# Wide expert rounds in blocks of 512, 1024, 1024 and 1024 inner columns, with extra and light tokens multiplied together

## What is computed

```python
def moe_swiglu(h, w_router, b_router, w1, w3, w2):
    logits = (h @ w_router) + b_router
    top_val, top_idx = lax.top_k(logits, TOP_K)          # TOP_K = 2
    top_w = softmax(top_val)
    gate = einsum('blk,blke->ble', top_w, one_hot(top_idx, N_EXPERTS))
    out = 0
    for e in range(N_EXPERTS):                            # 8
        out += gate[..., e:e + 1] * ((silu(h @ w1[e]) * (h @ w3[e])) @ w2[e])
    return out
```

## Time and profile before

| what | value |
|---|---|
| runs, median (3 runs) | 2324.79 us (2324.08 to 2325.15) |
| profiled execution, span from first to last instruction | 2321.8 us |
| profiled execution, time of its own | not given apart from the span; the median lies 3.0 us above the span |
| TensorE busy | 2176.6 us (94%) |
| TensorE weight loads | 1533.7 us (66%) |
| VectorE, ScalarE busy | 1193.5 us (51%), 788.2 us (34%) |
| DMA, mean rate | 278 GB/s |
| mean granted TensorE clock | 0.984 |
| loads of expert weights | 336 of 1024 KB, median 13.6 us from issue to landing |

### The profile page before, as it was taken

How to read it: one execution, slowest core, us unless ns; L and a number is a source line. 1 busy time by engine, 2 the same in 40 slices (tenths; PEclk the granted TensorE clock), 3 DMA queues, 4 the chain that set the end, 5 groups by cost and what they waited for, 6 DMA issues and landing times.

```text
span 2321.8 us, 40892 instructions
## 1 busy us (share of the span) xinstructions
PE 2176.6 (94%) x17031; PEld 1533.7 (66%) x17031; DVE 1193.5 (51%) x1899; ACT 788.2 (34%) x1195; POOL 223.8 (10%) x257
## 2 busy tenths in 40 slices
PE   7998999999988899999998999999999999889998
PEld 2974679976422233237776776687769987546997
DVE  3727847646501001015545464485557668984663
ACT  2511744433000000014344443344545542104552
POOL 1006310001000000000000000000000054660000
PEclk9998999999899999999999999999999999999999
DMA  9529387767999999999999999974667556505552
GB/s 344 171 90 290 86 294 247 281 210 289 388 415 407 414 403 409 414 404 355 394 394 363 346 394 392 378 229 147 221 215 253 182 192 226 236 10 183 191 190 73
DMA packets 254874, 645.38 MB, mean 278 GB/s; under 512 B 12831, under 2 KB 103136, under 8 KB 234600
## 3 DMA queue, kind: packets, MB, share of 16 engines
q1 hardware_dynamic: 248508, 629.93, 74.0%
q0 software_dynamic: 5904, 12.36, 2.1%
q10 hardware_dynamic: 284, 0.54, 0.1%
HBM read 641.72 MB, written 1.05 MB: 277 GB/s over the span
## 4 chain that ended last, share of the span: by engine, by line
PE 68%; DMA 19%; DVE 8%; issue 3%; ACT 1%; POOL 0%; SPq 0%; DVEq 0%; ACTq 0%; POOLq 0%
DMA ring<-in_moe_w 17%; PE bank L2003 6%; PE bank L2004 6%; PE bank L2005 6%; PE bank L2013 5%; PE bank L2015 5%; PE bank L2014 5%; PE bank L1039 3%; PE bank L887 3%; PE bank L1040 2%; PE bank L1041 2%; PE bank L1971 2%; PE bank L1949 2%; DVE arena L1761 2%; PE bank L933 2%
## 5 line engine op out<-in xcount | busy, mean ns | idle before, releaser
L1479 DVE TENSOR_TENSOR w_low<-ring,w_high 128x1024 fp32r<-128x1024 f32 x168 | 198.8, 1221 | 192.5 <-ACT w_high L1205 192.4
L3071 DVE TENSOR_TENSOR ring_low<-ring,up_high 128x1024 fp32r<-128x1024 f32 x186 | 224.7, 1265 | 115.9 <-ACT up_high L2628 115.6
L1205 ACT ACTIVATE w_high<-ring 128x1024 fp32r<-128x1024 f32 x168 | 170.0, 1054 | 246.7 <-DMA ring<-in_moe_w 216.6
L2628 ACT ACTIVATE up_high<-ring 128x1024 fp32r<-128x1024 f32 x186 | 182.6, 1046 | 85.1 <-PE bank L2015 72.5
L2003 PE MATMUL bank<-ht_low_cf_up,up_high 128*128 128x256 f32 x640 | 180.5, 282 | 0.0
L2004 PE MATMUL bank<-ht_high_cf_up,up_high 128*128 128x256 f32 x640 | 180.0, 281 | 0.0
L2005 PE MATMUL bank<-ht_high_cf_up,ring_low 128*128 128x256 f32 x640 | 178.0, 278 | 0.0
L822 PE MATMUL bank<-ring,arena 128*64 128x512 f32 (+1 forms) x512 | 109.9, 567 | 22.8 <-DMA ring<-in_moe_w 22.2
L2004 PEld LDWEIGHTS bank<-ht_high_cf_up,up_high 128*128 128x128 f32 x640 | 120.8, 189 | 0.1
L2005 PEld LDWEIGHTS bank<-ht_high_cf_up,ring_low 128*128 128x128 f32 x640 | 120.4, 188 | 0.0
L2003 PEld LDWEIGHTS bank<-ht_low_cf_up,up_high 128*128 128x128 f32 x640 | 120.1, 188 | 0.1
(11 more groups left out here) (543 smaller groups left out, 4636.3 us busy)
## 6 DMA issues: line engine op xcount, KB each, us to landing
ring<-in_moe_w SPq DMA_DIRECT2D x336, 1024.0 KB, 13.6
ring<-in_w_ada SPq DMA_DIRECT2D x48, 1024.0 KB, 5.0
ring<-in_ada_w SPq DMA_DIRECT2D x48, 1024.0 KB, 6.5
ring<-in_ffn_w_up SPq DMA_DIRECT2D x44, 1024.0 KB, 5.1
ring<-in_ffn_w SPq DMA_DIRECT2D x33, 1024.0 KB, 6.9
ring<-in_ret_w_in SPq DMA_DIRECT2D x24, 1024.0 KB, 5.4
ring<-in_ffn_w_down SPq DMA_DIRECT2D x22, 1024.0 KB, 5.0
ring<-in_w_in SPq DMA_DIRECT2D x12, 1024.0 KB, 10.9
```

Of the source, the lines that this page charges most:

```text
L1205: act.activation(WH[half % SPLIT][:, :], slot(moe_first + i)[:, HALF * (q % 2):HALF * (q % 2) + HALF], ACT.Copy)\
L1479: dve.tensor_tensor(out=WL[half % SPLIT][:, :], in0=slot(i)[:, HALF * (q % 2):HALF * (q % 2) + HALF], in1=WH[half % SPLIT][:, :], op=ALU.s ...
L2628: act.activation(high_of(part, n), slot(i)[:, HALF * q:HALF * q + HALF], ACT.Copy).then_inc(sem("up_high"), 1)
L3071: dve.tensor_tensor(out=low_of(i, q), in0=slot(i)[:, HALF * q:HALF * q + HALF], in1=high_of(part, n), op=ALU.subtract).then_inc(sem("up_lo ...
```

## The change

Wide rounds take the blocks of the mid rounds: w1, w3 and w2 of one block of 512 and three of 1024 inner columns. The ring order within a block becomes H0 L0 H1 L1 and so on (block 0: L0 L1 H0 H1 for w1, then for w3). Main work of a block of 1024 sums into two banks (w1: 0 and 1; w3: 2 and 7). The extra and the light tokens of a pair of tiles are multiplied in one go, `few_tokens`: column groups 0 and 2 hold the extra tokens, 1 and 3 the light ones, all in one bank, with 512 columns a matmul (256 in block 0), and both tiles are released together. The hidden values of both share one tile and one transpose. The end of the round has one half scatter in place of four quarter ones, and its start has four gate transposes, not six. On VectorE `gated_main` stands behind three splits of the next w1 block and `gated_few` behind the fourth. In the diff a line "..." marks what is left out; buffers that only move are left out.

```diff
 def pair_order():
-    order = [("L", kind, 0, h) for kind in ("w1", "w3") for h in range(2)]
-    order += [("H", kind, 0, h) for kind in ("w1", "w3") for h in range(2)]
-    for c in range(1, MOE_STEPS):
-        for kind, chunk in (("w1", c), ("w2", c - 2), ("w3", c)):
-            if 0 <= chunk < MOE_CHUNKS:
-                order += [(who, kind, chunk, h) for who in "HL" for h in range(2)]
+    order = [(who, kind, 0, h) for kind in ("w1", "w3") for who in "LH" for h in range(2)]
+    for s in range(1, BLOCK_STEPS):
+        for kind, block in (("w1", s), ("w2", s - 2), ("w3", s)):
+            if 0 <= block < len(NARROW_BLOCKS):
+                order += [(who, kind, block, h) for h in range(block_tiles(block)) for who in "HL"]
...
+                src = ...rearrange("(p k) n -> p k n" if n == 2 or tiles is pair_list else "(k p) n -> p k n", k=2)
...
+                def few_tokens(kind, s, h):
+                    chunks = NARROW_BLOCKS[s][1]
+                    ks = 2 if kind == "w2" else 4 // chunks
+                    at_h, at_l = (pair_at[who, kind, s, h] for who in "HL")
+                    tile_landed(pe, g, at_h)
+                    tile_landed(pe, g, at_l)
+                    both = [(XGX, cols_of(moe_first + at_h, ks)), (XGF[:, :, 0:EXTRA], cols_of(moe_first + at_l, ks))]
+                    for k in range(ks):
+                        for n in range(2):
+                            for y, (tokens, w) in enumerate(both):
+                                o = 64 * n + 32 * y
+                                if kind == "w2":
...
+                                else:
+                                    cols = SEQ * chunks
+                                    mm = pe.matmul(few(kind, s)[o:o + 32, :], tokens[:, ks * h + k, :], w[:, k, cols * n:cols * n + cols], ...
...
+                def turn_hidden(s):
+                    pe.wait_ge(sem("moe_hid"), r * MOE_CHUNKS + block_upto(s))
+                    chunks = NARROW_BLOCKS[s][1]
+                    for b in range(2 * chunks):
...
+                    for b in range(4 * chunks):
...
+                def tiles(kind, s, turned=None):
+                    together = 2 if turned is not None or (kind, s) == ("w3", 1) else 1
+                    main(kind, s, 0)
                     if turned is not None:
                         turn_hidden(turned)
+                    for h in range(1, together):
+                        main(kind, s, h)
+                    if turned is not None:
+                        pe.wait_ge(sem("hid_turned"), r * MOE_CHUNKS + block_upto(turned))
+                    if kind == "w3":
+                        pe.wait_ge(sem("moe_silu"), r * MOE_CHUNKS + block_upto(s))
+                    for h in range(block_tiles(s)):
+                        if h >= together:
+                            main(kind, s, h)
+                        few_tokens(kind, s, h).then_inc(sem("tile_used"), 2)
...
                 for kind in ("w1", "w3"):
+                    few_tokens(kind, 0, 0).then_inc(sem("tile_used"), 1)
+                    few_tokens(kind, 0, 1).then_inc(sem("tile_used"), 1)
+                    if kind == "w1":
+                        gates_to_rows(r, PGW, PGF, None)
                     for h in range(2):
+                        main(kind, 0, h, release=True)
...
-                scatter_quarter(PGTX, YEX, 0, False)
-                scatter_quarter(PGT[:, 1, :], YEN[:, 0:SEQ], 0, False).then_inc(sem("part_scattered"), 2)
...
-                scatter_quarter(PGTX, YEX, 1, False)
-                scatter_quarter(PGT[:, 1, :], YEN[:, 0:SEQ], 1, True).then_inc(sem("scattered"), 1)
+                scatter_half(PGT[:, 1, :], YEN, False, True).then_inc(sem("scattered"), 1)
...
 # ScalarE
+                for s in range(1, BLOCK_STEPS):
+                    if s < BLOCKS:
+                        split("w1", s, 0, 6)
+                        hidden_high(s - 1)
+                        split("w1", s, 6)
...
+                        split(*middle, 0, 4)
+                        if s < BLOCKS:
+                            silu(s)
+                        split(*middle, 4)
...
 # VectorE
+                for s in range(1, BLOCK_STEPS):
+                    if s < BLOCKS:
+                        split("w1", s, 0, 3)
+                        gated_main(s - 1)
+                        split("w1", s, 3, 4)
+                        gated_few(s - 1)
+                        split("w1", s, 4, 6)
+                        hidden_low(s - 1)
+                        split("w1", s, 6)
+                    middle = ("w2", s - 2) if s >= 2 else ("w3", s)
...
+                    if 2 <= s < BLOCKS:
+                        split("w3", s)
+                    if s == 2:
                         next_pick(r, g + 2)
```

More of the change, by code:

```diff
@@ L699, in block_load, with pair_load @@
             ins.then_inc(sa.landed[j % RING], 16)
-        def mid_load(sp, light, heavy, i):
-            who, kind, s, h = mid_list[i]
+        def pair_load(sp, tiles, light, heavy, i):
+            who, kind, s, h = tiles[i]
             e = light if who == "L" else heavy
@@ L907, in scatter_quarter, with scatter_half @@
                 return mm
-            def scatter_half(gates, y, first):
+            def scatter_half(gates, y, first, last=False):
                 for t in range(TT):
@@ L913, in scatter_half @@
                         mm = pe.matmul(bank(4 + 2 * t + n), gates[64 * n:64 * n + 64, P * t:P * t + P], y[64 * n:64 * n + 64, :],
-                                       start=first, stop=False)
+                                       start=first, stop=last)
                 return mm
@@ L1025, in wide @@
             def wide(j, p, r, g):
[L1026 to L1036, removed]
-                            first, last = k == 0, k == KD - 1
-                        cols = slice(BANK * m, BANK * m + BANK)
-                        pe.matmul(bank(b), low[:, k, :], w_high[:, cols], start=first, stop=False)
-                        pe.matmul(bank(b), high[:, k, :], w_high[:, cols], start=False, stop=False)
-                        mm = pe.matmul(bank(b), high[:, k, :], w_low[:, cols], start=False, stop=last)
-                    mm.then_inc(sem("w_used"), 1)
@@ L1196, in wide, with split @@
             def wide(j, p, r, g):
-                def split(kind, c, first=0, last=4):
-                    for q in range(first, last):
-                        half = half_of(kind, c, q)
-                        i = pair_at["H", kind, c, q // 2]
+                def split(kind, s, first=0, last=None):
+                    for q in range(halves(s))[first:last]:
+                        half = half_of(kind, s, q)
+                        i = pair_at["H", kind, s, q // 2]
                         if q % 2 == 0:
@@ L1472, in wide, with split @@
             def wide(j, p, r, g):
-                def split(kind, c, first=0, last=4):
-                    for q in range(first, last):
-                        half = half_of(kind, c, q)
-                        i = moe_first + pair_at["H", kind, c, q // 2]
+                def split(kind, s, first=0, last=None):
+                    for q in range(halves(s))[first:last]:
+                        half = half_of(kind, s, q)
+                        i = moe_first + pair_at["H", kind, s, q // 2]
                         dve.wait_ge(sem("w_high"), j * HALVES + (half + 1))
```

308 lines of the change are left out of this document (138 added, 170 removed).

## The result

The changed kernel takes 2348.68 us (median of 4 runs, 2345.09 to 2349.29) against 2324.97 for the kernel before beside it: 1.0096 times as long (95% interval 1.0083 to 1.0108), 23.7 us slower. The profiled execution took 2345.09 us, with a span of 2343.1 and a mean granted clock of 0.978 (before 0.984). Its span is 21.3 us longer than the one of before.

A forecast was written before the change was run, and what follows sets the result against it. TensorE was busy 94%, with DMA behind its 19.3 us of waits. Round +2.6 less 0.8, +3.6 for both, clock 5.1: +8.7 on span 2321.8, 2330.5; plus 3.0 to the median: 2333.5 us, range 2304 to 2348.

The forecast's parts named there:

- the likelier case: Waits at the block borders come as forecast and the kernel is slower; own range 2324 to 2346 us, chance 0.50.
- the border step: At a block's border the transposes wait for gated_few behind H1: TensorE stands some 5 us, costing DMA 4 us.
- Longer rows: Weight loads in a wide round: 214.4 us of DMA against 223.0, 8.6 us less if DMA never rests.
- The rival in which the rows bring nothing: Weight tiles in wide rounds take 0.12 us more than reckoned, +8 us a round: 2349 us, chance 0.07.
- Few-token matmuls: TensorE's joint extra and light tokens take 1.87 us a pair, against 1.89 before: nothing gained.
- The rival at 2460: Four groups of 512 columns on one bank don't overlap: 1.87 us more for each of 84 pairs; chance 0.03.
- Transposes: On TensorE twelve take 1.4 us; a round has 4.9 us of them against 5.2 before: nothing gained.
- The clock: TensorE's low clock after border stands: half of 1.7 us lost at each of six, 5.1 us in all.
- next_pick: Its 6.6 us on VectorE, now covered by one light tile instead of two: costed at nothing; bare, 3 us a round.
- The milestones: Reckoned times in the second wide round: H1 landings at 63.4, 118.3 and 183.0 us, end at 224.4 us.
- DMA gets ahead: At block 1's first release DMA rests less, H1 lands in time, all waits go: 2304 us, chance 0.28.

The follow-up runs named there:

- the kernel without stands: Changed kernel with gated_main and gated_few behind two splits, ScalarE's hidden_high behind four, next_pick at the start of the round: 2310.5 us, ratio 0.9937.
- the filler: Changed kernel with 20 more matmuls of 128x512 between main(0) and the transposes of blocks 2 and 4 only: 2337.03 us, ratio 1.004.
- The first experiment: Changed kernel with VectorE's gated_main and gated_few behind two splits of the next block instead of three and four: 2330.72 us, ratio 1.0021.

## Why the forecast was right in its direction and too small in its size

Forecast were 2333.5 us and measured 2348.68: slower, as the likelier case (0.50) had it, but by 23.7 us where 8.7 were reckoned. That is above the 2324 to 2346 of this case and at the upper end of the whole range, 2348 (just past it by the median, just inside by the ratio, 2347). The slowdown comes from the wait that the border step describes, as shown below; its size was forecast 15 us too small.

**Longer rows: right.** The stretches without a stand move 409 to 413 GB/s, as read from the mid round, and with the short rows back 386 to 394. By the forecast's own prices 48 tiles of 2.72 instead of 2.56 us are 7.7 us a round; 3.3 to 4.4 were measured, in a kernel whose DMA does not run through everywhere (the dip at the start stays). The 214.4 us that a round of DMA was put at is near what the kernel without stands comes to, 215.0 and 218.0 us; the closeness of the first is partly luck, since its DMA still dips near the start. The rule of the Trainium skill that was weighed against this step ("DMA: Bandwidth & Descriptors", Specifications) would have had these kernels equal; the runs disagree. The rival in which the rows bring nothing has nearly the right time, 2349, for a reason that did not happen.

**Few-token matmuls: right.** A price of 1.87 us a pair was forecast from the chain of waits. The chain of the changed kernel:

```profile
1067.50 1.85 PE bank L1033 x16
...
1072.35 1.85 PE bank L1033 x16
```

The rival at 2460 falls with these. **Transposes: right at full clock.** Twelve took 1.46 us with the filler (1102.20 to 1103.66), 1.4 was forecast; at the low clock 2.5. The half scatter took 1.99 us, forecast 1.85.

**The wait at the border: right.** H1 of block 2 landed 62.6 us into the round (63.4 forecast), the turn came 5.3 us later (5.5), TensorE stood 4.98 us (4.7 to 5). From the turn to the release of the first slots 6.3 us were reckoned; with the filler, at full clock, it is 6.25 (1102.20 to 1106.63, and half of 3.64). The first experiment shows that this wait is the cause: 18 of the 23.7 us go with the order of three calls on VectorE, and 31 with ScalarE's copy as well.

**The clock: this term of the sum was sized wrong.** The forecast took "half, 0.85 x 6 = 5.1". Where TensorE stands ahead of the transposes, four times in all, 2.6 us are measured in TensorE's rows and 2.9 to 3.3 in the time. At block 3 the stand of 3.59 us likewise brought the low clock, and main(0) took 5.3 us instead of 2.98, but that cost next to nothing. The changed kernel there, VectorE and TensorE in order of time:

```profile
1161.82 0.68 DVE L1487 TENSOR_TENSOR HT<-HT,bank 128x512 f32<-128x512 f32 x1
```

```profile
1162.64 0.95 PE L1043 MATMUL bank<-ident,HT 128*128 128x128 f32 x4
...
1167.25 3.64 PE L1033 MATMUL bank<-ring,arena 128*32 128x512 f32 x32
```

`gated_few` ends at 1162.50, and the transposes begin at 1162.64. At full clock main(0) would have been done 2.3 us earlier, and the transposes would have waited for `gated_few` all the same. From them to the few tokens it is 4.61 us, against 4.43 with the filler at block 2. So the low clock cost some 0.3 us there. The six borders together cost four times 2.6 to 3.3 and twice 0.3, 11 to 14 us where 5.1 were taken: 6 to 9 of the 15 us by which the forecast was short.

The step had two faults. Between a case with no loss (2.69 us idle) and one with 1.7 (5.34 us) it took the middle, though 4.7 lies next to the upper one. And it took 1.7 us as the upper one from a round start, where 3.5 us passed at the low clock; behind the first of these stands it was 5.9. Neither figure is fixed. In the kernel with next_pick at the start alone, six stands of 4.86 to 5.01 us are followed by 5.6 to 6.2 us from the transposes to the few tokens (5.95 in the rows above, 1164.80 to 1170.75), so by a loss of 1.2 to 1.8 us; its clock was low for 6.8 us at two of the six and for 3.4 at the others, that of the changed kernel for 6.8 at all six. A price of this kind taken from one execution can be off by about 1 us a stand.

**next_pick: costed at nothing, and half right.** The forecast named its bare price, 3 us a round, and the stand is there, 3.6 us. But it didn't come on top: it takes the place of the border's own wait (two experiments moved it and gained nothing). Only with the gates mended is it worth 6 us, both rounds with their clock. That makes the cover named in the forecast wrong and its zero nearly right, for a reason that the forecast did not give.

**The milestones.** From the start of the round, forecast and measured: H1 of block 2 63.4 and 62.6, of block 3 118.3 and 121.8, of the last border 183.0 and 188.7, the end 224.4 and 234.1. The first stretch is 0.8 short, the three that hold a border are 4.3, 2.2 and 4.0 over; the clock, which these milestones left out, explains about 2.6 of the first and the last and 0.3 of the middle one. What is left, 1.7, 1.9 and 1.4, with the -0.8 ahead of them, is 4.2 us a round, 8 in both. No experiment looked for it: about half of the 15 us lies there, and its cause stays open.

**The rivals.** "DMA gets ahead" at 2304 was given 0.28. Its ground was that so little decides at block 2; its place was wrong. In no run with the gates as they were did H1 come early enough, as the forecast's own reckoning had it. What it would have brought is seen where the waits were taken away by reordering: 2310.5.

**A new wait in the place of one removed** was met in each step. Early gates uncovered ScalarE's copy (18 us gained, 13 still held); the early copy alone gave nothing; next_pick alone gave nothing; with all three no wait within a round is over 1.2 us.

## What to carry to other kernels

When a tile becomes larger, look at every handshake that was put "after so many tiles of the next block": a product that needs nothing of the next weights must not stand in a queue behind the second tile that is still to land, on any of the engines that take part, and the mending shows in full only when it is done on all of them. A stand of TensorE costs itself and, behind it, the low clock for the work that releases the buffers; if DMA is the limit, both reach the end of the kernel. Where the next step waits for another engine anyway, as at block 3, the low clock costs almost nothing: ask which wait ends last before you count it. A value between two rows of a trace is not their middle, and a price read from one execution needs a second.

## What the runs showed of the hardware that was not expected

- Stands of TensorE of 3.6 and 5.0 us within a stream were all followed by a granted clock of 1.2 GHz, in the changed kernel for 5.2 to 6.1 us of work, longer than the 3.5 us seen behind 5.34 us of idle time at a round's start; behind equal stands in the kernel with next_pick at the start alone it was low for 3.4 us at four of six.
- The length of a single stand did not decide it: 2.39 us in the first experiment brought the low clock, 2.69 us in the kernel before did not.
- 20 matmuls that nobody needs, placed in each of four such stands, kept the clock at 2.4 GHz there and made the kernel 11.7 us faster.
- Four column groups in one bank with 512 columns each take 1.85 us for 16 records, against 1.87 for 8 records with two groups; here the number of groups added nothing.
